# Reordering the start of a two-model transformer kernel: when weights are loaded, how a norm gets its statistics, and where side work stands

## The reference

```python
x_lat = layer_norm(x, ln_in_g, ln_in_b)            # the first norm: x and ctx, 512 tokens
x_ctx = layer_norm(ctx, ln_in_g, ln_in_b)
silu_c, silu_cc = jax.nn.silu(c), jax.nn.silu(c_ctx)
for l in range(DEPTH):                              # DEPTH = 2
    sh1, sc1, g1, sh2, sc2, g2 = split(silu_c @ w_mod[l] + b_mod[l], 6)     # modulation
    a_lat = x_lat * (1 + sc1) + sh1                 # "modulated" input of the mixer
    ...
    f, nq, nk, nv, cq, ckv, kr, g = split(h @ w_in) # the mixer's projections; nv are the values
    ...
    out = sum_over_3_branches(sigmoid(gate) * (y_branch @ w_branch)) @ w_out
    x_lat = layer_norm(ALPHA * x_lat + (1 + g1) * m_lat, ln1_g[l], ln1_b[l])
    f_lat = swiglu(x_lat * (1 + sc2) + sh2, w_ffn_gate[l], w_ffn_up[l], w_ffn_down[l])
    x_lat = layer_norm(ALPHA * x_lat + (1 + g2) * f_lat, ln2_g[l], ln2_b[l])
```

## Time and profile before

| | |
|---|---|
| median of 3 runs | 2131.55 us (2127.8 to 2150.82) |
| the profiled execution's own time | 2127.88 us |
| its span, first to last instruction | 2126.1 us |
| TensorE busy | 1969.0 us (93%) |
| VectorE busy | 1281.8 us (60%) |
| ScalarE busy | 848.6 us (40%) |
| mean granted TensorE clock | 0.970 of full speed |
| loaded from HBM | 329.31 MB, 155 GB/s over the span |

### The profile page before, as it was taken

One profiled execution on the slowest core, in us unless ns is written; L12 is line 12 of the kernel. 1 busy time (PEld: TensorE's weight loads), 2 busy tenths in 40 slices (PEclk: granted clock), 3 DMA queues, 4 the chain that ended last, 5 costly groups with the idle time before them and its releaser, 6 DMA issues.

```text
span 2126.1 us, 32028 instructions
## 1 busy us (share of the span) xinstructions
PE 1969.0 (93%) x12468; PEld 1626.4 (76%) x12468; DVE 1281.8 (60%) x2174; ACT 848.6 (40%) x1366; POOL 129.0 (6%) x110
## 2 busy tenths in 40 slices
PE   5999989998999999999898988989997899988998
PEld 3776657546768788887687664879997889987998
DVE  6512454564447567677634566666667777666775
ACT  4422353253234122222433445354445754444444
POOL 0000000000030001204000000020111100000000
PEclk9999999999999999999999999999997999998999
DMA  9642513105553556546465140856662446652664
GB/s 328 188 139 82 175 40 94 50 1 181 176 184 123 203 183 200 196 158 218 129 216 167 62 134 2 283 194 196 199 196 90 150 146 193 189 167 81 205 193 137
DMA packets 280758, 332.07 MB, mean 156 GB/s; under 512 B 13190, under 2 KB 229692, under 8 KB 280508
## 3 DMA queue, kind: packets, MB, share of 16 engines
q1 hardware_dynamic: 268608, 323.05, 46.6%
q10 hardware_dynamic: 12028, 7.32, 1.3%
HBM read 329.31 MB, written 1.05 MB: 155 GB/s over the span
## 4 chain that ended last, share of the span: by engine, by line
PE 75%; DVE 8%; issue 6%; DMA 5%; ACT 4%; POOL 1%; SPq 1%; DVEq 0%; ACTq 0%; POOLq 0%
PE ps L550 20%; PE ps L551 19%; PE ps L552 19%; PE ps L1341 3%; DVE SL L509 2%; PE ps L1367 2%; PE ps L368 2%; DMA RAW<-in_w_in 2%; PE ps L1351 2%; ACT SH L503 1%; DMA RAW<-in_w_out 1%; PE ps L947 1%; PE ps L1576 1%; DMA EARLY<-in_w_mod 1%; DMA RAW<-in_w_branch 1%
## 5 line engine op out<-in xcount | busy, mean ns | idle before, releaser
L509 DVE TENSOR_TENSOR SL<-RAW,SH 128x1024 fp32r<-128x1024 f32 (+2 forms) x448 | 524.5, 1174 | 431.1 <-ACT SH L503 426.4
L550 PE MATMUL ps<-AB,SH 128*128 128x256 f32 (+1 forms) x1984 | 644.6, 325 | 40.2 <-DVE AB L1077 22.6
L551 PE MATMUL ps<-AB,SH 128*128 128x256 f32 (+1 forms) x1984 | 637.2, 321 | 0.0
L552 PE MATMUL ps<-AB,SL 128*128 128x256 f32 (+1 forms) x1984 | 636.7, 321 | 0.0
L503 ACT ACTIVATE SH<-RAW 128x1024 fp32r<-128x1024 f32 (+2 forms) x448 | 443.6, 997 | 423.4 <-PE ps L552 269.0
L550 PEld LDWEIGHTS ps<-AB,SH 128*128 128x128 f32 x1984 | 378.2, 191 | 94.4 <-issue 34.5
L552 PEld LDWEIGHTS ps<-AB,SL 128*128 128x128 f32 x1984 | 378.9, 191 | 29.2
L551 PEld LDWEIGHTS ps<-AB,SH 128*128 128x128 f32 x1984 | 378.1, 191 | 27.5
L550 PE MATMUL ps<-HH,SH 128*128 128x256 f32 (+1 forms) x992 | 304.5, 307 | 3.5 <-DVE HL L779 1.6
L551 PE MATMUL ps<-HL,SH 128*128 128x256 f32 (+1 forms) x992 | 302.4, 305 | 0.0
L552 PE MATMUL ps<-HH,SL 128*128 128x256 f32 (+1 forms) x992 | 302.4, 305 | 0.0
(11 more groups left out here) (286 smaller groups left out, 2176.8 us busy)
## 6 DMA issues: line engine op xcount, KB each, us to landing
SIDE<-in_w_mod SPq DMA_DIRECT2D x45, 2048.0 KB, 8.0
RAW<-in_ffn_w SPq DMA_DIRECT2D x64, 1024.0 KB, 5.4
RAW<-in_w_in SPq DMA_DIRECT2D x44, 1024.0 KB, 6.1
RAW<-in_w_ffn_gate SPq DMA_DIRECT2D x22, 1024.0 KB, 9.0
RAW<-in_w_ffn_up SPq DMA_DIRECT2D x22, 1024.0 KB, 5.4
RAW<-in_w_ffn_down SPq DMA_DIRECT2D x16, 1024.0 KB, 5.8
RAW<-in_w_branch SPq DMA_DIRECT2D x24, 512.0 KB, 3.5
RAW<-in_w_out SPq DMA_DIRECT2D x8, 1024.0 KB, 6.7
```

The lines of the kernel that those rows point to most:

```text
L509: e.tensor_tensor(SL[:, m, 0:kt, :], RAW[p][:, 0:kt, o:o + P], SH[:, m, 0:kt, :].bitcast(F32), ALU.subtract).then_inc(K.up("weight_low"), 1)
L550: e.matmul(ps, SH[:, m, k, :], xh, start=k == 0, stop=False)
L551: e.matmul(ps, SH[:, m, k, :], xl, start=False, stop=False)
L552: ins = e.matmul(ps, SL[:, m, k, :], xh, start=False, stop=k == self.kt - 1)
```

## The change

Five things are changed.

1. In the opening, SyncE issues RAW0, chunk 0, chunk 1, RAW1, chunk 2, chunk 3; before it was RAW0, RAW1 and then the four chunks.
2. The first norm's statistics are taken on columns, as in the other norms: `add_columns` in place of the full rows, small operations on 128x4, then `diagonals` and `pe_spread`, which stands on TensorE between the rows of chunk 0 and those of chunk 1. On ScalarE the root goes ahead of all four weight splits. On VectorE the split of m-tile 1 goes behind the first `centre`. The turn of chunk 2, the rows and the turn of chunk 3 move to other places in the first unit, and its flips and adds with them.
3. In every norm that feeds a modulated input, scale and shift are folded (`DER` rows 2+s and 8+s hold gain times scale, and bias times scale plus shift), ScalarE makes the modulated tile from `NT` first and writes `X` after it. `prep_scales` has eight small VectorE operations for two streams, before two; the opening does it in two halves and signals `half_ready` after the second, which ScalarE waits for at k=4.
4. `Values` does its last token tile in halves too, and signals `values_half` after the first; ScalarE then splits m-tiles 0 and 1 of the next unit, reads the last tile, and splits 2 and 3.
5. In `Branch`, `pe_rows` stands at the start of m-tile 2, and `flip` ahead of reading m-tile 2.

```diff
@@ class Unit
+        rows_tile = 3
-                if self.side and (m, k) == (3, 0) and not self.by_k:
+                if self.side and (m, k) == (self.rows_tile, 0) and not self.by_k:
                     self.side.pe_rows(e, K, 0)
...
-                if self.side and m == self.side.flip_at and not (self.by_k or self.hold):
+                if self.side and m == (self.rows_tile if self.rows_tile < 3 else self.side.flip_at) and not (self.by_k or self.hold):
                     self.side.flip(e, K, 0)
@@ class Values
-                halves = [(0, 2), (2, 4)] if t == 0 else [(0, 4)]
+                halves = [(0, 2), (2, 4)] if t in (0, 3) else [(0, 4)]
...
+                    if (t, m0) == (3, 0):
+                        ins.then_inc(K.up("values_half"), 1)
...
         def act(self, e, K):
-            for m in range(4):
+            for m in range(3):
                 e.wait_ge(sem["products"], K.at("products", m + 1))
                 self.read_act(e, K, m)
-            for m in range(4):
+            e.wait_ge(sem["values_half"], K.at("values_half", 1))
+            for m in (0, 1):
+                self.nxt.split_act(e, K, m, 2)
+            e.wait_ge(sem["products"], K.at("products", 4))
+            self.read_act(e, K, 3)
+            for m in (2, 3):
                 self.nxt.split_act(e, K, m, 2)
@@ class Branch
+        rows_tile = 2
@@ class Norm, act: this block now stands ahead of the one that writes X, and reads t in place of X
+                if self.to == "a":
+                    if k >= 2:
+                        e.wait_ge(sem["input_low"], K.at("input_low", k - 1))
+                    if self.split and k == 0:
+                        e.wait_ge(sem["dve_done"], K.at("dve_done"))
+                    if self.opening and k == KT // 2:
+                        e.wait_ge(sem["half_ready"], 1)
+                    for s, c in enumerate(range(c0, c1, SEQ)):
+                        last = c + SEQ == c1
+                        at = c - c0
+                        e.activation(A32[:, k % 2, c:c + SEQ], t[:, at:at + SEQ], ACT.Identity,
+                                     bias=self.sh(s, k), scale=self.sc(s, k)) \
+                            .then_inc(K.up("modulated" if last else "act_done"), 1)
@@ class Opening
-        ROWS = (4, 7)
+        ROWS = (4, 3, 4, 4)
...
-            self.unit.load(e, K)
             for j, c in enumerate(self.CHUNKS):
+                if j != 1 and j < 3:
+                    p = j // 2
+                    e.dma_start(RAW[p][:, 0:KT, :], self.unit.src(K, p)).then_inc(K.up(f"pair{p}_loaded", 16), 16)
                 e.dma_start(self.places[j][:, :, :], rows(wmod[0])[:, :, c * 512:(c + 1) * 512]) \
                     .then_inc(K.up(f"chunk{j}_loaded", 16), 16)
...
-            for m in range(2):
-                self.unit.split_act(e, K, m, 1)
             self.norm.act_root(e, K)
-            for m in range(2, 4):
+            for m in range(4):
                 self.unit.split_act(e, K, m, 1)
...
-            e.tensor_scalar(MU[:, :], PS[6][:, :], 1.0 / D, None, ALU.mult).then_inc(K.up("dve_done"), 1)
...
+            self.norm.dve_var(e, K)
+            self.norm.dve_rstd(e, K)
             self.flip(e, K, 0)
             self.unit.split_dve(e, K, 0)
-            self.unit.split_dve(e, K, 1)
             self.flip(e, K, 1)
             self.add(e, K, 0)
-            e.wait_ge(sem["root_done"], K.at("root_done", 1))
-            e.reciprocal(RSTD[:, :], VAR[:, :]).then_inc(K.up("dve_done"), 1)
             self.add(e, K, 1)
             self.prep(e, K, 0)
             e.wait_ge(sem["dve_done"], K.own("dve_done"))
+            e.wait_ge(sem["spread_done"], K.at("spread_done", 2))
             self.norm.centre(e, K, 0)
-            self.unit.split_dve(e, K, 2)
+            for m in (1, 2):
+                self.unit.split_dve(e, K, m)
             self.norm.centre(e, K, 1)
...
-                e.matmul(PS[6][:, :], ONES[:, :], X[:, k, :], start=False, stop=k == KT - 1)
+                self.norm.add_columns(e, 6, 4, X[:, k, :], False, False)
...
             self.rows_of(e, K, 0)
+            K.bank[6] = K.bank[7] = ("var_done", K.s("var_done") + 1)
+            self.norm.pe_spread(e, K)
             self.rows_of(e, K, 1)
...
+            if (m, k) == (2, 0):
+                self.turn(e, K, 2)
             if (m, k) == (0, 1):
-                self.turn(e, K, 2)
                 self.rows_of(e, K, 3)
-            if (m, k) == (2, 1):
+            if (m, k) == (0, 2):
                 self.turn(e, K, 3)
@@ def prep_scales, inner f
-                e.tensor_scalar(DER[:, 2 + s, :], mod(mat, chunk_sc, s), 1.0, 1.0 / alpha, ALU.add, ALU.mult) \
+                e.tensor_scalar(DER[:, 2 + s, t], mod(mat, chunk + 1, s)[:, t], 1.0, 1.0 / alpha, ALU.add, ALU.mult) \
                     .then_inc(K.up("dve_done"), 1)
+            e.wait_ge(sem["dve_done"], K.own("dve_done"))
+            for s in range(streams):
+                e.tensor_tensor(DER[:, 8 + s, t], DER[:, 2 + s, t], DER[:, 1, t], ALU.mult).then_inc(K.up("dve_done"), 1)
+            e.wait_ge(sem["dve_done"], K.own("dve_done"))
+            for s in range(streams):
+                e.tensor_tensor(DER[:, 8 + s, t], DER[:, 8 + s, t], mod(mat, chunk, s)[:, t], ALU.add) \
+                    .then_inc(K.up("dve_done"), 1)
+                e.tensor_tensor(DER[:, 2 + s, t], DER[:, 2 + s, t], DER[:, 0, t], ALU.mult).then_inc(K.up("dve_done"), 1)
```

More of the change, by code:

```diff
@@ L1104, in act_root @@
             e.wait_ge(sem["var_done"], K.at("var_done", 1))
[L1105 removed]
+            var = SM[:, 0:len(self.blocks())]
             e.activation(var, var, ACT.Sqrt).then_inc(K.up("root_done"), 1)
@@ L1122, in act @@
                     e.activation(A32[:, k % 2, c0:c1], X[:, k, c0:c1], ACT.Square).then_inc(K.up("normed_squared"), 1)
-                if self.to == "a":
-                    if k >= 2:
-                        e.wait_ge(sem["input_low"], K.at("input_low", k - 1))
-                    src = t
-                    if self.write_x:
-                        e.wait_ge(sem["x_normed"], K.own("x_normed"))
-                        src = X[:, k, c0:c1]
-                    if self.split and k == 0:
-                        e.wait_ge(sem["dve_done"], K.at("dve_done"))
-                    for s, c in enumerate(range(c0, c1, SEQ)):
-                        last = c + SEQ == c1
-                        at = c - c0
-                        e.activation(A32[:, k % 2, c:c + SEQ], src[:, at:at + SEQ], ACT.Identity,
-                                     bias=self.sh(s, k), scale=self.sc(s, k)) \
-                            .then_inc(K.up("modulated" if last else "act_done"), 1)
+            if self.write_x:
+                e.wait_ge(sem["x_normed"], K.own("x_normed"))
         def pool(self, e, K):
@@ L1765, in prep @@
         def prep(self, e, K, half):
-            t = slice(4 * half, 4 * half + 4)
-            e.wait_ge(sem["side_added"], K.own("side_added"))
-            for s in range(2):
-                e.tensor_scalar(DER[:, 2 + s, t], mod(0, 1, s)[:, t], 1.0, 1.0 / ALPHA, ALU.add, ALU.mult) \
-                    .then_inc(K.up("dve_done"), 1)
+            prep_scales(ALPHA, 0, 0, 2, slice(4 * half, 4 * half + 4))(e, K)
         def dve_between(self, e, K, k):
@@ L1839, in pe @@
             e.wait_ge(sem["copied_out"], K.at("copied_out", 3))
-            e.matmul(PS[6][:, :], ONES[:, :], S1[:, :], start=True, stop=False)
+            self.norm.add_columns(e, 6, 4, S1[:, :], True, False)
             for k in range(4, KT):
```

64 lines of the change are left out of this document (30 added, 34 removed).

## The result

The changed kernel takes **2123.66 us** (median of 15 runs, 2115.53 to 2133.03), the kernel before **2141.7 us** (15 runs on the same chips, 2127.8 to 2150.95). The ratio is 0.9918, 95% interval 0.9898 to 0.9939: some 17.5 us faster. The forecast was 16.4 us less, and 2113 us, with a range up to 2122. So the gain has the size that was forecast and the time has not: the number from which the gain was taken off, 2127.88 us, is near the fastest that the kernel before does, and not its middle.

What follows compares the result with a forecast made beforehand. TensorE, busy 1969.0 of 2126.1 us, bounds the kernel, so only its waits can be won. Terms 1.0 + 4.8 + 3.4 + 5.5 + 1.7 = 16.4 us off 2127.88 give 2111.5, raised to 2113 us; range 2105 to 2122.

Steps and rivals of the forecast that it cites:

- The base: Whole kernel: gain taken off the profiled execution's 2127.88 us, plus part of the 3.7 us the three-run median lay above.
- Opening, -1.0: Opening, at the first matmul: plain sum of the chain's terms -1.25 us, taken as -1.0, ends 0 and -2.6.
- The reciprocal: Opening, VectorE: the 128x512 reciprocal becomes 128x4, so the second add comes earlier, -2.6 us.
- the added split: Opening, VectorE: another weight split ahead of the second centre delays ScalarE's first modulated tile, +1.15 us.
- the load order: Opening: chunk 1 lands ahead of RAW1; alone worth at most 2.7 us, here 0.5 at chunk 1's rows.
- the fourth rival: Opening stands at 0, new spread eating the earlier landing, split and scales the reciprocal; 2112.5 to 2116 us, chance 0.15.
- Values, -4.8: Behind both Values units: last tile in halves lets splits start early, -2.4 us each, ends -4.2 and -5.0.
- The clock behind Values, -3.4: Behind both Values units: half-clock stretches vanish with the gap, 1.7 us each, ends 0 and -3.4.
- The rival that the clock gives nothing back: Behind Values: slow stretches are chance or stay, so gain is 13.0 us, 2114.9 to 2118 us; chance 0.2.
- Third branch, -5.5: Third branch's two turns: earlier flip removes TensorE waits of 2.43 and 3.31 us, ends -3.0 and -5.74.
- No row waits for SIDE: Branch: SIDE lands 3.3 us before the moved rows; rival that they stall TensorE, 2134 us, chance 0.03.
- Norms, -1.7: Layer 0's two norms: modulated tile no longer waits for X, -0.84 us each; layer 1 nothing; ends -0.8 and -2.3.

Runs made afterwards that it cites:

- the two edits alone: Kernel before with only the last Values tile in halves and the branch's rows and flip moved to m-tile 2: 2125.65 us (6 runs), ratio 0.9918.

## Why the prediction missed, point by point

**The base: this is the step that failed.** "The median of the three runs lies 3.7 us above that execution; I take a part of it", says the prediction. That part was 1.5 us; over 15 runs the median lies 13.8 us above that execution. The profiled execution (2127.88) and the smallest of the three runs are the bottom of a spread; the medians of 12 to 19 runs are 2137.74 to 2143.15. From 2141.7 the forecast gain gives 2125.3, 1.6 above the measured 2123.66. The three runs shown (2127.80, 2131.55, 2150.82) had 23 us between them, and that alone should have widened the range upwards: a sum made against one execution forecasts a difference.

**Opening, -1.0: wrong in sign, a mis-sized term.** The reciprocal, the added split, the small operations and the cover of X's write came as worked out; the load order took the 2.00 us wait away, and nothing came of it. What was missing is the price of the column sums, which the forecast took for free: they end at the low clock, and so chunk 0's rows take 1.6 to 1.7 us more, in all but one trace the sums another 0.7 to 2.7 us. In the first pair this is most of it: chunk 1's rows start 1.9 us later than forecast (31.75 for 29.85), 1.57 of them by the slow rows of chunk 0, and the first matmul 1.8 us later (43.16 for the 41.36 of its sum). The term is +2.2 to +2.5 us on the mean of five traces. A sign of it stood in the trace of the kernel before. These are the column sums of layer 0's norm behind the mixer in it, with the clock low from 623.4 on, so that each narrow matmul takes 0.23 us in place of 0.12:

```profile
621.18 1.95 PE L947 MATMUL ps<-ONES,S 128*128 128x1 f32 x16 [1.88 <-POOL S L799]
622.99 1.47 PE L947 MATMUL ps<-ONES,X 128*128 128x1 f32 x8
624.33 1.85 PE L947 MATMUL ps<-ONES,NT 128*128 128x1 f32 x8
```

In both norms of layer 0 a low clock begins beside these sums in all 14 traces, 28 times of 28; a wait of 1.9 to 2.0 us stands ahead of them there, so they alone would not have told narrow work from the wait. The opening does.

The title's part does nothing by itself (the fourth rival): undone, it moves neither first matmul (42.24 against 42.19, 46.28 against 46.15 to 46.49).

**Values, -4.8: right.** The halving costs +0.31 and +0.16. The rows had given 0.33, from layer 0. The Trainium skill, "TensorE: Matmul & The Clock Gate", Back-to-back issue gap, gives 0.06 us by estimate; for layer 0 the measurement decides for the rows, and in layer 1, with the same widths, 0.16 lies between the two.

**The clock behind Values, -3.4: right in this pair**, and a matter of chance in one place of the six with the gap. The rival that the clock gives nothing back falls. With the gap kept the low clock was absent behind one of two units of one trace, and the trace agrees with what the Trainium skill says there (the same page, Part 1 on the clock gate): where the clock changes varies from run to run.

**Third branch, -5.5: right.** -5.88 in the pair, 5.14 by undoing it alone. No row waits for SIDE, not even a tile earlier.

**Norms, -1.7: too large.** The mechanism is there, at about 0.5 us a norm instead of 0.84, about 1 us in all; the pair showed -0.25 over steps of 101 and 303 us, under the scatter of the clock stretches there (at the first norm 10.2 us in one and 6.8 us in the other).

**The sum.** By single undoings and repeated traces: opening +2.2 to +2.5, Values -6.9 to -8.4, branch -5.0 to -5.9, norms about -1. That is -10.5 to -13 us against some 17.5 measured, and the two middle terms alone gave 17.5 as well (0.9918). Between 4.5 and 7 us are therefore not placed. The interval of the ratio, 13 to 22 us, touches the upper end of that sum; whether the rest is that uncertainty or fewer low-clock stretches later is left open. So it is in part luck that the total came near 16.4: the opening missed by over 3 us and the norms by 0.7 us on one side, and as much or more is unexplained on the other. Two places show how much the traces scatter away from the edits. Behind the last turn (L324 at 1423.59 in the kernel before), for the most part the second block, the 14 traces take 697.7 to 714.7 us. And from the turn at 251.06 to the one at 358.14 the two traces of the kernel before take 107.1 and 107.6 us, the twelve others 107.1 to 116.8 us, the longest with a low clock of 17 us from about 253 on. That is layer 0's first attention, which no edit touches; whether an edit ahead of it brings this on or it is chance was not tested.

## What to carry to other kernels

Take a forecast gain off the median of many runs, and where there are three with 23 us between them, widen the range by that. An edit that frees one engine in an opening is worth only what the next late thing leaves: look for the last wait before the first real matmul, and count what is queued ahead of it. Before trading wide matmuls for narrow ones, look at what TensorE runs next and at which granted clock.

## What the runs showed of the hardware

- The same program's executions differ by 27 us (2127.59 to 2155.14 us). Two traces of the kernel before have spans of 2126.1 and 2146.0 us with 127.1 and 164.6 us of low clock, added up from the granted clock. Half of the 37.5 us between them, 18.8, is nearly all of the 19.9 us. It is no rule: the kernel with the two edits alone had 183.5 us of low clock and a span of 2129.7. That such stretches cost little where TensorE waits anyway would explain it, and is not shown.
- Narrow f32 matmuls (128x1, 0.12 us each at full clock) in a stretch that TensorE fills with gaps of at most 0.3 us were met by the low clock in eight traces of eight (from 23.0 to 26.1 us on, sums from 20.2 to 29.3), although the engine was busy nearly all the time; with 128x512 ones in their place or between them, in none of six (five and one).
- A gap of 2.78 us was followed by 3.4 us at half clock in five of six places.
